# Expert loop of a mixture-of-experts layer: rows gathered in quarters, block transposes on VectorE, weight rows loaded in a matching order

## The chip, the cores and the metric

The kernel runs on one core of a Trainium2 chip. Its time is the device time of one execution in microseconds (us), median of several runs.

## The reference

One layer on 1024 tokens of width 1024, all in float32. A dense part (modulation from `c`, RMSNorm, an input projection, a gated linear recurrence, a spatial gating unit, an output projection) gives `h`. Then a mixture of 32 experts, 4 per token:

```
logits = hf @ router_w + router_b;  top 4 of 32, softmax over the four = gates
gu = xb @ w_gu[e] + b_gu[e]                    # xb: the rows of expert e, w_gu[e]: 1024 x 2048
g, lin = split(gu); g = min(g, 7); lin = clip(lin, -7, 7)
act = g * sigmoid(1.702 * g) * (lin + 1)
y = act @ w_down[e] + b_down[e]                # w_down[e]: 1024 x 1024
out[token] += y * gate
```

The sum is scaled by `g2`, added to `h`, and a last RMSNorm follows. The weights of the experts are 32 x (8 + 4) MiB = 402.65 MB; each expert's are read once.

## The kernel before

The dense part fills the first part of the run. At its end the router's results give a list of **items**: one item is up to 128 rows of one expert, cut into up to four **units** of 32 rows. With the reference's inputs the 32 experts have 8, 8, 5, 10, 4, 8, 7, 5, 3, 4, 1, 2, 2, 2, 3, 3, 5, 1, 4, 2, 4, 3, 4, 3, 5, 5, 2, 3, 4, 5, 12 and 6 units: 143 units in 47 items (so 15 items beyond the first of an expert, in 13 of the experts). Each engine runs a loop over the 47 items.

**TensorE, one item.** Weights are the moving operand, and a unit's 32 rows are the stationary one, so four 32-column matmuls stand side by side in the array, each on another quarter of the output columns. `gate_and_linear(u, half)` (line 1117) multiplies unit `u` with the slabs 0 to 3 or 4 to 7 of `w_gu` (a slab is 128 rows of the matrix), `down(u, ...)` (line 1143) with the eight of `w_down`. The item's 128 rows were gathered from `hs_rows` as whole rows of 4 KB, so they stand with tokens on partitions: `transpose_rows` (line 1084) turns them by eight TensorE transposes into PSUM, and ScalarE's `modulate` (line 780) drains them into `izT` with scale and shift. The activation of a unit is turned the same way (`transpose_act`, line 1129, drained by `drain_at`, line 792). `make_list` (line 1062) finds the tokens of an item by a product with a one-hot matrix, `repeat_rows` (line 1071) copies token number and gate to the four quarters of the partitions.

**VectorE** reads the list (`read_list`), builds the one-hot matrix (`make_onehot`, line 1567), adds biases and clamps (lines 1620 to 1628), multiplies the activation (line 1631) and scales the result (lines 1636, 1639). **ScalarE** takes the sigmoid (line 787). **GpSimd** issues the gather of the next item (line 577), multiplies gate and sigmoid (line 594), and issues per unit a scatter that adds into `acc_rows` (line 587), each behind the landing of the one before.

**SyncE** loads the weights. All 12 loads of an expert are 1 MiB: eight slabs of `w_gu` (`chunk_source`, rows `q*128` to `q*128+127`), then four of `w_down` with two slabs each. There is room for one expert's weights alone, so the loads are released in three groups by `freed[0..2]`, counted in items: the slabs 0 to 3 when the first matmul of the second half of the expert's last item has run, the slabs 4 to 7 with the first `down` of that item, the down slabs with the `repeat_rows` behind its last `down`. The loads of the first expert start within the dense part: slabs 6 and 7 and the down slabs come last of them. At the very start SyncE issues eleven small loads of parameters (line 395), each a matrix of so many rows of 128 numbers, one row per partition:

```
PARAM_ROWS = [("c", 8), ("norm1_g", 8), ("norm2_g", 8), ("conv_b", 4), ("lru_br", 4), ("lru_bi", 4),
              ("lru_lambda", 4), ("gnorm_lru_g", 4), ("gnorm_sgu_g", 4), ("conv_w", 16), ("ada_b", 48)]
```

Of the kernel before, what the change touches and what calls it, by code (L numbers as in the profile page):

```python
# [14 lines left out]
BF16 = mybir.dt.bfloat16  # L15
# [46 lines left out]
CHUNKS = 12  # L62
# [3 lines left out]
BIAS = 768  # L66

# [65 lines left out]
def build(nc, ins, out):  # L133
# [8 lines left out]
    with ExitStack() as ctx:  # L142
# [37 lines left out]
        zg = r2[:, 0:1024]  # L180
        izT = r2[:, 1024:2048].rearrange("p (k n) -> p k n", k=KT)
        actT = r2[:, 2048:3072].rearrange("p (u h n) -> p u h n", u=UMAX, h=2)
        act_sb = r2[:, 3072:3584].rearrange("p (b n) -> p b n", b=2)
        gate_sb = r2[:, 3584:4096].rearrange("p (b n) -> p b n", b=2)
        lin_sb = r2[:, 4096:4608].rearrange("p (b n) -> p b n", b=2)
        sig_sb = r2[:, 4608:5120].rearrange("p (b n) -> p b n", b=2)
        gsig_sb = r2[:, 5120:5632].rearrange("p (b n) -> p b n", b=2)
        y_sb = r2[:, 5632:6656].rearrange("p (u n) -> p u n", u=UMAX)
        bias_rows = r2[:, 8192:8192 + 2 * BIAS]
        onehot = r2[:, 9728:10240].bitcast(BF16).rearrange("p (t n) -> p t n", t=TT)  # L190
        repeat = r2[:, 10240:10752].rearrange("p (u i n) -> p u i n", u=UMAX, i=4)
        g2_rows = r2[:, 10752:11008]
        lgT_sb = r2[0:NE, 12288:13312]
# [26 lines left out]
        scale2 = sb("scale2", [P, KT])  # L220
# [18 lines left out]
        slot_c = sb("slot_c", [P, 2])  # L239
        quarter = sb("quarter", [P, 1])  # L240
        lst = g1row[:, 372:378]
        lst_t = g1row[:, 380:384]
        cur6 = g1row[:, 384:408].bitcast(BF16).rearrange("p (t i) -> p t i", t=TT)
        row_gate = g1row[:, 408:410]
        idx_next = sb("idx_next", [P, 1], I32)
        sidx_next = sb("sidx_next", [P, UMAX], I32)
        sidx_cur = sb("sidx_cur", [P, UMAX], I32)
        sgate_next = g1row[:, 416:420]
        sgate_cur = g1row[:, 420:424]
# [61 lines left out]
        pair_made = sem("pair_made")  # L311
        freed = [sem(f"freed{c}") for c in range(3)]
        z1_made = sem("z1_made")
        z2_made = sem("z2_made")
        z1_drained = sem("z1_drained")
        z2_drained = sem("z2_drained")
# [9 lines left out]
        at_drained = sem("at_drained")  # L326
# [63 lines left out]
        def _(sp_):  # L390
# [25 lines left out]

            def bias_in_rows(e):
# [11 lines left out]
            for q in range(CHUNKS):  # L429
# [7 lines left out]
                if q == 10:  # L437
                    sp_.wait_ge(filled, JOB[("rank", 0)] + 1)
                sp_.dma_start(chunk_tile(q), chunk_source(0, q)).then_inc(w_arrived[q], SEMW)
# [3 lines left out]
            for e in range(1, NE):  # L443
                done = sp_.value_load(items_i[0:1, CUM_ITEMS + e - 1:CUM_ITEMS + e], min_val=1, max_val=MAX_ITEMS)
                for q in range(CHUNKS):
                    if q % 4 == 0:
                        sp_.wait_ge(freed[q // 4], done)
                    sp_.dma_start(chunk_tile(q), chunk_source(e, q)).then_inc(w_arrived[q], SEMW)
# [25 lines left out]
        def _(pool):  # L474
            chain = [0]

            def link(ins_):
# [22 lines left out]
            link(pool.iota(tokpart[:, :, 0], pattern=[[1, TT]], base=-TT, channel_multiplier=0,  # L500
                           allow_small_or_imprecise_dtypes=True))
            link(pool.iota(tokpart[:, :, 1], pattern=[[0, TT]], base=0, channel_multiplier=1,
                           allow_small_or_imprecise_dtypes=True))
            link(pool.memset(tokpart[:, :, 2], 1.0))
            link(pool.iota(slot_c[:, 0:1], pattern=[[0, 1]], base=S, channel_multiplier=1,
                           allow_small_or_imprecise_dtypes=True))
            link(pool.iota(slot_c[:, 1:2], pattern=[[0, 1]], base=0, channel_multiplier=-1,
                           allow_small_or_imprecise_dtypes=True))
            for i in range(4):
                link(pool.memset(quarter[32 * i:32 * i + 32, :], float(i)))  # L510
# [1196 lines left out]
```

## Time and profile before

| what | value |
|---|---|
| median of 3 runs | 2426.13 us (2425.0 to 2430.72) |
| the profiled execution | 2432.23 us, its span 2430.5 us |
| granted TensorE clock, mean | 0.947 |
| TensorE matmuls busy | 2136.2 us, 88% of the span |
| VectorE, ScalarE, GpSimd busy | 769.7, 388.2, 440.6 us |
| moved by DMA | 525.82 MB, mean 216 GB/s |

The span is cut into 40 slices in the profile. The expert loop fills it from 523.5 us (the first matmul of line 1117) to 2398.3 us. Times below are microseconds from the start of the span. A TensorE instruction on float32 leaves two records, so 32 matmuls of a unit with `w_gu` stand as 64.

### The profile page before, as it was taken

Reading aid. Unit: us, or ns where it says so; the run is one execution under the profiler, and the core shown is the slowest. Engines: PE = TensorE matmul, PEld = TensorE weight load, DVE = VectorE, ACT = ScalarE, POOL = GpSimd, SP = SyncE. Lnnn points to the kernel's source line nnn. Section 1 sums busy time; section 2 is a strip of 40 time slices with the busy share of each in tenths; the row PEclk is TensorE's granted clock in tenths of the full one; section 3 lists DMA queues with packets and bytes.
Section 4 is the critical chain, followed back from the end, with each engine's and each line's share of the span. In section 5 each row is a group of like instructions: output and inputs, shape, how many; then the busy total and the mean of one; then the engine's idle time right before and its main releaser. Section 6 shows DMA issues by size and latency. Waiting matters only on the chain.

```text
span 2430.5 us, 53256 instructions
## 1 busy us (share of the span) xinstructions
PE 2136.2 (88%) x21037; PEld 924.2 (38%) x21038; DVE 769.7 (32%) x2033; ACT 388.2 (16%) x866; POOL 440.6 (18%) x420
## 2 busy tenths in 40 slices
PE   3998989959998999999796799797898889989994
PEld 3443444424433343443343233333343333433342
DVE  6437554232222232222222222222222222222223
ACT  3044112211011111101011101101101111010112
POOL 2000030112222121221211111111121111122121
PEclk9999999969999999999898899898999989999997
DMA  9312224323464357436799997699787549944245
GB/s 337 121 39 104 104 113 164 105 93 123 132 242 163 96 189 286 147 110 237 251 366 369 401 398 277 247 388 356 270 317 264 204 167 406 360 132 160 88 162 166
DMA packets 142462, 525.82 MB, mean 216 GB/s; under 512 B 14672, under 2 KB 45376, under 8 KB 109664
## 3 DMA queue, kind: packets, MB, share of 16 engines
q1 hardware_dynamic: 111728, 470.39, 49.9%
q0 software_dynamic: 30704, 55.06, 10.2%
q8 instruction: 15, 0.25, 0.0%
q14 instruction: 15, 0.12, 0.0%
HBM read 493.02 MB, written 32.37 MB: 216 GB/s over the span
## 4 chain that ended last, share of the span: by engine, by line
PE 58%; DMA 19%; issue 9%; DVE 6%; SPq 2%; ACT 2%; POOL 2%; POOLq 1%; DVEq 0%; ACTq 0%
PE psum L1117 29%; PE psum L1143 12%; DMA acc_rows<-r,sidx_cur 10%; PE psum L1013 4%; PE psum L880 4%; DMA r<-hs_rows,idx_next 4%; DMA big<-in_exp_w_gu_dram 3%; PE psum L975 2%; PE psum L1084 1%; PE psum L1129 1%; DMA big<-in_w_in_dram 1%; PE psum L1071 1%; POOL r L594 1%; PE psum L922 1%; DMA big<-in_exp_w_down_dram 1%
## 5 line engine op out<-in xcount | busy, mean ns | idle before, releaser
L1117 PE MATMUL psum<-big,r 128*32 128x512 f32 x9152 | 1022.0, 600 | 23.5 <-DMA big<-in_exp_w_gu_dram 23.0
L1143 PE MATMUL psum<-big,r 128*32 128x256 f32 x9152 | 529.2, 385 | 17.2 <-issue 14.2
L1117 PEld LDWEIGHTS psum<-big,r 128*32 128x32 f32 x9152 | 286.5, 111 | 675.7 <-issue 632.0
L1143 PEld LDWEIGHTS psum<-big,r 128*32 128x32 f32 x9152 | 293.7, 111 | 227.6 <-issue 54.2
L587 POOL DMA_INDIRECT acc_rows<-r,sidx_cur x143 | 229.0, 1601 | 804.8 <-DMA acc_rows<-r,sidx_cur 435.6
L787 ACT ACTIVATE r<-r 128x256 f32<-128x256 f32 x143 | 59.4, 416 | 1252.7 <-DVE r L1626 1252.7
L594 POOL TENSOR_TENSOR r<-r 128x256 f32<-128x256 f32 x143 | 104.5, 731 | 647.9 <-ACT r L787 647.8
L1620 DVE TENSOR_TENSOR r<-psum,r 128x256 f32<-128x256 f32 x143 | 60.7, 425 | 505.3 <-PE psum L1117 505.3
L1636 DVE TENSOR_TENSOR r<-psum,r 128x256 f32<-128x256 f32 x143 | 60.8, 425 | 437.0 <-PE psum L1143 437.0
L1084 PE MATMUL psum<-ident,r 128*128 128x128 f32 x384 | 70.7, 315 | 129.1 <-DMA r<-hs_rows,idx_next 129.1
L880 PE MATMUL psum<-r,big 128*128 128x512 f32 x384 | 167.8, 597 | 1.5 <-DMA big<-in_w_in_dram 1.5
L780 ACT ACTIVATE r<-psum,mod,scale 128x128 f32<-128x128 f32 x384 | 142.1, 461 | 28.0 <-PE psum L1084 28.0
L1631 DVE TENSOR_TENSOR r<-r 128x256 f32<-128x256 f32 x143 | 60.8, 425 | 215.9 <-POOL r L594 215.9
L792 ACT ACTIVATE r<-psum 128x256 f32<-128x256 f32 x143 | 55.3, 386 | 377.1 <-PE psum L1129 377.1
L1084 PEld LDWEIGHTS psum<-ident,r 128*128 128x128 f32 x384 | 50.4, 160 | 169.5 <-DMA r<-hs_rows,idx_next 142.7
L1013 PE MATMUL psum<-big,r 128*128 128x512 f32 x256 | 111.1, 594 | 0.5 <-DMA big<-in_w_out_dram 0.3
L880 PEld LDWEIGHTS psum<-r,big 128*128 128x128 f32 x384 | 73.2, 191 | 92.9 <-issue 91.2
L1013 PEld LDWEIGHTS psum<-big,r 128*128 128x128 f32 x256 | 48.3, 190 | 62.5 <-issue 61.3
L1639 DVE SCALAR_TENSOR_TENSOR r<-r,g1row 128x256 f32<-128x256 f32 x143 | 69.5, 486 | 5.1
L1129 PE MATMUL psum<-ident,r 128*128 128x128 f32 x286 | 63.0, 304 | 6.6 <-DVE r L1631 6.6
L1268 DVE SCALAR_TENSOR_TENSOR gacc<-big,cact,gacc 128x512 f32<-128x512 f32 x84 | 63.2, 752 | 3.0
L577 POOL DMA_INDIRECT r<-hs_rows,idx_next x48 | 48.7, 1015 | 69.0 <-DVE idx_next L1587 44.0
(233 smaller groups left out, 1122.5 us busy)
## 6 DMA issues: line engine op xcount, KB each, us to landing
big<-in_exp_w_gu_dram SPq DMA_DIRECT2D x256, 1024.0 KB
big<-in_exp_w_down_dram SPq DMA_DIRECT2D x128, 1024.0 KB
big<-in_ada_w_dram SPq DMA_DIRECT2D x12, 2048.0 KB, 12.9
r<-in_x_dram SPq DMA_DIRECT2D x16, 512.0 KB, 12.5
big<-in_w_in_dram SPq DMA_DIRECT2D x4, 2048.0 KB, 19.1
r<-in_exp_b_gu_dram SPq DMA_DIRECT2D x128, 64.0 KB
big<-in_w_out_dram SPq DMA_DIRECT2D x2, 2048.0 KB, 13.3
hs_rows<-r POOLq DMA_DIRECT2D x8, 512.0 KB, 3.2
```

Source lines behind the costliest of these rows:

```text
L587: pool.indirect_dma_start(acc_quarters, bass.IndirectOffsetOnAxis(ap=sidx_cur[:, u:u + 1], axis=0), y_sb[:, u, :], None, bounds_check=4 * ...
L594: pool.tensor_tensor(gsig_sb[:, u % 2, :], gate_sb[:, u % 2, :], sig_sb[:, u % 2, :], ALU.mult).then_inc(gsig_made, 1)
L780: ins_ = act.activation(izT[:, k, :], psum[:, 6 + half, i * P:(i + 1) * P], ACT.Identity, bias=mod[:, SH2 + k:SH2 + k + 1], scale=scale2[: ...
L880: last = pe.matmul(b, w[:, k, m * P:(m + 1) * P], zT[:, k, th * 512:(th + 1) * 512], start=(k == 0), stop=(k == KT - 1))
L1013: last = pe.matmul(b, src[:, ct % CT, t * P:(t + 1) * P], ring(("wout", dh))[:, ct, :], start=(ct == 0), stop=(ct == 2 * CT - 1))
L1084: last = pe.transpose(psum[:, 6 + half, i * P:(i + 1) * P], zg[:, k * P:(k + 1) * P], ident[:, :])
L1117: last = pe.matmul(psum[32 * j:32 * j + 32, u, :].rearrange("p (a n) -> p a n", a=2), izT[:, k, u * UNIT:(u + 1) * UNIT], rhs[:, :, 256 * ...
L1129: last = pe.transpose(psum[:, u, h * P:(h + 1) * P], act_sb[:, u % 2, h * P:(h + 1) * P], ident[:, :])
L1143: ins_ = pe.matmul(psum[32 * i:32 * i + 32, 4 + u % 2, 0:256], actT[:, u, h, 32 * j:32 * j + 32], down_slab(f)[:, 256 * i:256 * i + 256], ...
L1268: ins_ = dve.scalar_tensor_tensor(out=a, in0=w[:, k, :], scalar=cact[:, k:k + 1], in1=a, op0=ALU.mult, op1=ALU.add)
L1631: dve.tensor_tensor(act_sb[:, u % 2, :], lin_u, gsig_sb[:, u % 2, :], ALU.mult).then_inc(act_made, 1)
L1639: dve.scalar_tensor_tensor(out=y_sb[:, u, :], in0=y_sb[:, u, :], scalar=sgate_cur[:, u:u + 1], in1=g2_rows, op0=ALU.mult, op1=ALU.mult).th ...
```

## The change

- A weight slab is now rows `k*32` to `k*32+31` of each of the four quarters of the matrix (`j` = 0 to 3 on partitions `32j` to `32j+31`), not 128 rows that follow each other. The source of a load has the shape 4 x 32 x 2048 (or 1024), the destination 128 partitions. The down slabs are loaded one by one: 16 loads per expert in place of 12.
- The gather of an item is four indirect DMAs, each of 128 quarter rows of 1 KB: partition `32i + n` of unit `u` gets quarter `i` of token `n`'s row. VectorE turns each 32 x 32 block of it by one instruction (`block_rows`), and ScalarE's `modulate` reads SBUF, with scale and shift rearranged once to match (`shift2`).
- Gate times sigmoid moves from GpSimd to VectorE, and a second block transpose there makes the operand of `down`; `transpose_rows`, `transpose_act` and `drain_at` are gone.
- Lists are made three items ahead and gathers issued two ahead; the scatters of an item no longer wait for each other, only for those of the item before.
- The slabs 4 to 7 are released by the first matmul of `make_list`, which now stands ahead of the `down` products.

```diff
-CHUNKS = 12
+CHUNKS = 16
...
         def chunk_tile(q):
-            if q < 8:
-                return gu_slab(q)
-            at = (q % 2) * 2048
-            return big[:, SLOT_OF_PAIR[q // 2], at:at + 2048].rearrange("p (k n) -> p k n", k=2)
+            return gu_slab(q) if q < 8 else down_slab(q - 8)
         def chunk_source(e, q):
             if q < 8:
-                return w_gu[e, q * P:(q + 1) * P, :]
-            return w_down[e, (q - 8) * 256:(q - 7) * 256, :].rearrange("(k p) n -> p k n", p=P)
+                return w_gu[e].rearrange("(j k r) n -> k j r n", j=4, k=KT)[q]
+            return w_down[e].rearrange("(j k r) n -> k j r n", j=4, k=KT)[q - 8]
...
+            def load_chunk(e, q):
+                sp_.dma_start(chunk_tile(q), chunk_source(e, q)).then_inc(w_arrived[q], SEMW)
...
+            def gather(turn, step):
                 pool.wait_ge(idx_made, turn + 1)
+                if not (isinstance(turn, int) and turn == 0):
+                    pool.wait_ge(z_blocked, turn)
                 pool.sem_inc(may_start, 1)
-                pool.indirect_dma_start(zg, None, hs_rows, bass.IndirectOffsetOnAxis(ap=idx_next[:, 0:1], axis=0)
-                                        ).then_inc(rows_in, SEMW)
+                step(pool.tensor_copy(gather_idx[:, :], quarter_of[:, bass.ds(turn * UMAX, UMAX)]))
+                pool.sem_inc(may_start, 1)
+                for u in range(UMAX):
+                    pool.indirect_dma_start(z_quarters[:, u, :], None, hs_quarters,
+                                            bass.IndirectOffsetOnAxis(ap=gather_idx[:, u:u + 1], axis=0)
+                                            ).then_inc(rows_in, SEMW)
...
+            def block_rows(turn):
+                dve.wait_ge(rows_in, turn * (UMAX * SEMW) + UMAX * SEMW)
+...
                dve.transpose(z_blocks.rearrange("p u k n -> p (u k n)"), z_quarters.rearrange("p u n -> p (u n)")
+                              ).then_inc(z_blocked, 1)
...
+                    dve.tensor_tensor(gsig_sb[:, u % 2, :], gate_u, sig_sb[:, u % 2, :], ALU.mult).then_inc(gsig_made, 1)
 XX_tensor(act_sb[:, u % 2, :], lin_u, gsig_sb[:, u % 2, :], ALU.mult).then_inc(act_made, 1)
+                    dve.transpose(actT[:, u, :, :].rearrange("p k n -> p (k n)"), act_sb[:, u % 2, :]).then_inc(at_made, 1)
...
-                transpose_rows(g + 1, 0)
-                transpose_act(0)
...
+                make_list(g + 3)
+                down(0)
                 load_item(g + 1)
```

SyncE's queue, the loads of the second expert. Before:

```order
L448 DMA big<-in_exp_w_gu_dram 128x2048 x4
L422 DMA r<-in_exp_b_gu_dram 32x2x256
L425 DMA r<-in_exp_b_down_dram 32x256
L422 DMA r<-in_exp_b_gu_dram 32x2x256
L425 DMA r<-in_exp_b_down_dram 32x256
L422 DMA r<-in_exp_b_gu_dram 32x2x256
L425 DMA r<-in_exp_b_down_dram 32x256
L422 DMA r<-in_exp_b_gu_dram 32x2x256
L425 DMA r<-in_exp_b_down_dram 32x256
L448 DMA big<-in_exp_w_gu_dram 128x2048 x4
L448 DMA big<-in_exp_w_down_dram 128x2x1024 x4
```

With the change:

```order
L421 DMA big<-in_exp_w_gu_dram 128x1x2048 x4
L428 DMA r<-in_exp_b_gu_dram 32x2x256
L431 DMA r<-in_exp_b_down_dram 32x256
L428 DMA r<-in_exp_b_gu_dram 32x2x256
L431 DMA r<-in_exp_b_down_dram 32x256
L428 DMA r<-in_exp_b_gu_dram 32x2x256
L431 DMA r<-in_exp_b_down_dram 32x256
L428 DMA r<-in_exp_b_gu_dram 32x2x256
L431 DMA r<-in_exp_b_down_dram 32x256
L421 DMA big<-in_exp_w_gu_dram 128x1x2048 x4
L421 DMA big<-in_exp_w_down_dram 128x1x1024 x8
```

The shapes are those of the destination; the order is the same, and the down slabs are eight loads.

TensorE, from the second half of an item's first unit to its first `down` product. Before:

```order
L1117 MATMUL psum<-big,r 32x512 x16
L350 UNCONDITIONAL_BRANCH
L1079 ISA
L1084 MATMUL psum<-ident,r 128x128 x4
L1107 REGISTER_ALU
L1129 MATMUL psum<-ident,r 128x128 x2
L348 COMPARE_AND_BRANCH
L348 UNCONDITIONAL_BRANCH
L1117 MATMUL psum<-big,r 32x512 x16
```

With the change:

```order
L1101 MATMUL psum<-big,r 32x512 x16
L355 UNCONDITIONAL_BRANCH x3
L1049 REGISTER_ALU
L1051 REGISTER_ALU
L1053 MATMUL psum<-g1row,r 128x6 x8
L1091 REGISTER_ALU
L1119 MATMUL psum<-big,r 32x256 x32
```

No transposes stand between the products any more, and the list's product stands ahead of `down`.

VectorE, one unit's activation. Before:

```order
L1620 TENSOR_TENSOR r<-psum,r 128x256
L1622 ISA
L1622 SCALAR_TENSOR_TENSOR r<-psum,r 128x256
L1626 TENSOR_SCALAR r<-r 128x256
L1628 TENSOR_SCALAR r<-r 128x256
L1631 TENSOR_TENSOR r<-r 128x256
```

With the change:

```order
L1585 TENSOR_TENSOR r<-psum,r 128x256
L1587 SCALAR_TENSOR_TENSOR r<-psum,r 128x256
L1591 TENSOR_SCALAR r<-r 128x256
L1593 TENSOR_SCALAR r<-r 128x256
L1596 TENSOR_TENSOR r<-r 128x256
L1598 TENSOR_TENSOR r<-r 128x256
L1600 STREAM_TRANSPOSE r<-r 128x256
```

The rows L1596 and L1600 are new on this engine.

## Rows read from the trace of the kernel before

**Rows 1.** The page: span and busy time.
```profile
span 2430.5 us, 53256 instructions
```
**Rows 2.** Groups by line on PE: shapes xcount | busy us, mean ns | idle before, releasers.
```profile
L1117 PE MATMUL psum<-big,r 128*32 128x512 f32 x9152 | 1022.0, 600 | 23.5 <-DMA big<-in_exp_w_gu_dram 23.0 <-issue 0.5
L1143 PE MATMUL psum<-big,r 128*32 128x256 f32 x9152 | 529.2, 385 | 17.2 <-issue 14.2 <-DMA big<-in_exp_w_down_dram 2.8
...
L1084 PE MATMUL psum<-ident,r 128*128 128x128 f32 x384 | 70.7, 315 | 129.1 <-DMA r<-hs_rows,idx_next 129.1
...
L1129 PE MATMUL psum<-ident,r 128*128 128x128 f32 x286 | 63.0, 304 | 6.6 <-DVE r L1631 6.6
```
**Rows 3.** Stretches: busy us per engine, PEclk, DMA share of 16 engines, GB/s.
```profile
530.00:2400.00 1870.00, 1696.69 (x19674) 712.57 (x19666) 494.49 (x1601) 241.32 (x662) 378.59 (x331) 0.96 0.66 238
```
**Rows 4.** Timeline of an undisturbed stretch: start, us, engine, line.
```profile
1112.85 7.11 PE L1143 MATMUL psum<-big,r 128*32 128x256 f32 x128 [0.33 <-issue]
...
1119.90 1.05 PE L1071 MATMUL psum<-g1row,r 128*128 128x2 f32 x8
...
1121.08 20.81 PE L1117 MATMUL psum<-big,r 128*32 128x512 f32 x192
```
**Rows 5.** DMA queues and issues, whole span.
```profile
q1 hardware_dynamic: 111728, 470.39, 49.9%
q0 software_dynamic: 30704, 55.06, 10.2%
...
big<-in_exp_w_gu_dram SPq DMA_DIRECT2D x256, 1024.0 KB
big<-in_exp_w_down_dram SPq DMA_DIRECT2D x128, 1024.0 KB
```
**Rows 6.** DMA in the first 10 us: packets by size, and four of the loads.
```profile
DMA packets 857, 1.42 MB, mean 142 GB/s; under 512 B 80, under 2 KB 192, under 8 KB 857
...
r<-in_norm_g_dram SPq DMA_DIRECT2D x2, 4.0 KB
r<-in_ada_b_dram SPq DMA_DIRECT2D x1, 24.0 KB
...
r<-in_conv_b_dram SPq DMA_DIRECT2D x1, 2.0 KB
...
r<-in_conv_w_dram SPq DMA_DIRECT2D x1, 8.0 KB
```
**Rows 7.** Stretch in which four slabs of weights land, columns as in rows 3.
```profile
604.00:608.00 4.00, 3.67 (x70) 2.03 (x64) 0.91 (x2) 0.07 (x1) 0.33 (x1) 1.00 1.01 426
```
**Rows 8.** Timeline of SyncE: last loads of expert 0, three groups of expert 1.
```profile
477.53 16.51 SPq L439 DMA_DIRECT2D big<-in_exp_w_down_dram  x4
...
586.02 2.10 SPq L448 DMA_DIRECT2D big<-in_exp_w_gu_dram  x4
...
601.72 2.13 SPq L448 DMA_DIRECT2D big<-in_exp_w_gu_dram  x4
617.06 2.02 SPq L448 DMA_DIRECT2D big<-in_exp_w_down_dram  x4
```
**Rows 9.** A two-unit item: stretch as in rows 3, and a TensorE wait.
```profile
1340.00:1365.00 25.00, 19.02 (x179) 5.96 (x171) 5.34 (x16) 4.18 (x12) 4.03 (x4) 0.86 1.03 407
...
1349.13 1.94 PE L1117 MATMUL psum<-big,r 128*32 128x512 f32 x8 [2.03 <-DMA big<-in_exp_w_gu_dram]
```
**Rows 10.** Timeline: the last work of the loop on TensorE.
```profile
2398.19 1.05 PE L1071 MATMUL psum<-g1row,r 128*128 128x2 f32 x8
```
**Rows 11.** Groups by line on DVE and POOL, columns as in rows 2.
```profile
L594 POOL TENSOR_TENSOR r<-r 128x256 f32<-128x256 f32 x143 | 104.5, 731 | 647.9 <-ACT r L787 647.8
...
L1631 DVE TENSOR_TENSOR r<-r 128x256 f32<-128x256 f32 x143 | 60.8, 425 | 215.9 <-POOL r L594 215.9
...
L1567 DVE TENSOR_TENSOR r<-r 128x1024 bf16 x49 | 60.1, 1226 | 3.1
...
L1395 DVE TENSOR_REDUCE r<-big 128x512 f32<-128x2048 f32 x3 | 10.9, 3669 | 2.0 <-ACT big L697 2.0
```

More of the change, by code:

```diff
@@ L66 @@
 BIAS = 768
+LISTS = MAX_ITEMS + 3
 def bank_jobs():
@@ L310, in build @@
         may_start = sem("may_start")
-        pair_made = sem("pair_made")
+        copy_made = sem("copy_made")
+        rows_repeated = sem("rows_repeated")
+        rows_taken = sem("rows_taken")
+        z_blocked = sem("z_blocked")
         freed = [sem(f"freed{c}") for c in range(3)]
[L313 to L316, printed above, removed]
+        z_made = [sem(f"z_made{c}") for c in range(2)]
+        affine2_made = sem("affine2_made")
+        shift2_made = sem("shift2_made")
         gu_made = sem("gu_made")
@@ L325, in build @@
         at_made = sem("at_made")
-        at_drained = sem("at_drained")
         dn_made = sem("dn_made")
@@ L609, in gsig_2 @@
-                def gsig_2():
-                    times_sigmoid(prior, 2)
-                    by_units(pool, units, 3, gsig_3)
-                def gsig_1():
-                    times_sigmoid(prior, 1)
-                    by_units(pool, units, 2, gsig_2)
-                by_units(pool, units, 1, gsig_1)
+                gather(g + 2, step)
+                pool.wait_ge(acc_out, prior * SEMW + SEMW * TT)
+                pool.sem_inc(may_start, 1)
+                step(pool.tensor_copy(scatter_idx[:, :], quarter_of[:, bass.ds(g * UMAX, UMAX)]))
@@ L737, in _ @@
             group_root(1, 1)
+            act.wait_ge(affine2_made, 1)
+            for j in range(4):
+                for q in range(4):
+                    ins_ = act.activation(shift2[32 * j:32 * j + 32, :, :].rearrange("p a (h q) -> p a h q", h=2)[:, :, :, q],
+                                          affine2[32 * q:32 * q + 32, :, 2 * j:2 * j + 2], ACT.Copy)
+            ins_.then_inc(shift2_made, 1)
             def norm_h(t):
@@ L775, in modulate @@
             def modulate(turn, half):
-                act.wait_ge((z1_made, z2_made)[half], turn + 1)
-                for i in range(4):
-                    k = 4 * half + i
-                    ins_ = act.activation(izT[:, k, :], psum[:, 6 + half, i * P:(i + 1) * P], ACT.Identity,
-                                          bias=mod[:, SH2 + k:SH2 + k + 1], scale=scale2[:, k:k + 1])
-                ins_.then_inc((z1_drained, z2_drained)[half], 1)
+                act.wait_ge(z_blocked, turn + 1)
+                for k in range(4 * half, 4 * half + 4):
+                    ins_ = act.activation(izT[:, k, :].rearrange("p (u n) -> p u n", u=UMAX), z_blocks[:, :, k, :],
+                                          ACT.Identity, bias=shift2[:, 1, k:k + 1], scale=shift2[:, 0, k:k + 1])
+                ins_.then_inc(z_made[half], 1)
             def sigmoid(prior, u):
@@ L1591, in _ @@
+            def block_rows(turn):
+                dve.wait_ge(rows_in, turn * (UMAX * SEMW) + UMAX * SEMW)
+                if not (isinstance(turn, int) and turn == 0):
+                    dve.wait_ge(z_made[0], turn)
+                    dve.wait_ge(z_made[1], turn)
+                dve.transpose(z_blocks.rearrange("p u k n -> p (u k n)"), z_quarters.rearrange("p u n -> p (u n)")
+                              ).then_inc(z_blocked, 1)
+            TAKE_STEPS = 5
             dve.wait_ge(gates_made, 1)
```

286 lines of the change are left out of this document (122 added, 164 removed).

## The prediction

> **What bounds the kernel now.** I read the groups by line first. TensorE is busy nearly all the time: the two expert products take 1022.0 and 529.2 us, and the transposes that the change removes take 70.7 + 63.0 us and have 129.1 + 6.6 us of waiting ahead of them, nearly all for the gather [rows 2]. The windows say the same of the loop: in 1870 us TensorE is busy 1697, VectorE 494, and the DMA engines 0.66 of their time [rows 3]. So the loop is bound by TensorE, but not by far: a DMA share of 0.66 with all 16 engines at work means that the weights could stand a slowdown of 1.5 and no more. In a two-unit item they bind already: the share is 1.03 at 407 GB/s, and TensorE waits 2.03 us for one slab [rows 9].
>
> So the first question is not what the transposes cost but whether the weights still come as fast. They are 402.65 MB, 384 loads of 1 MiB [rows 5].
>
> **How a load is spread over the engines.** The first 10 us show eleven small loads: three of 8 rows (`c` and the two norms), six of 4 rows (as `conv_b`), one of 16 (`conv_w`), one of 48 (`ada_b`) [rows 6]. Their data are 112 packets of 512 B, which is 192 - 80 in the packet line; the 80 packets under 512 B are their completions, one per engine that took part [rows 6]. Eleven loads on 16 engines each would leave 176. 3 x 8 + 6 x 4 + 16 + 16 = 80 fits exactly. So a load whose outermost count is 4 ran on four engines, one of 8 on eight, one of 48 on sixteen. Before the change every weight load has 128 outermost on both sides. With it the source is 4 x 32 x 2048: the outermost count is 4 on the source's side, 128 on the destination's. No row shows such a mixed pair. Either the smaller one decides, and a load has 4 engines, or the larger, and it has 16. I take 4: a share for an engine must be cut from both sides alike, and 4 blocks that do not follow each other cannot be cut 16 ways along their outermost step.
>
> The Trainium skill states this as a rule ("DMA: Bandwidth & Descriptors", "Why a DMA increments its semaphore by 16 and not by 1"): the largest number up to 16 that divides the slowest dimension of both sides, and from SyncE the lowest-numbered engines. By that rule, with which the 80 completions agree, the weight loads all share the same four. Which engines a load takes, no row here shows.
>
> **The sum if a weight load has four engines.**
> - The rate of one engine: 426 GB/s at a share of 1.01 of 16 [rows 7] is 26.4 GB/s, so four give 105.4. The lower bound is the mean of the whole queue, 470.39 MB in 49.9% of 16 engines' 2430.5 us [rows 5, 1], 24.2 GB/s. I take 26.4, since it comes from weight slabs alone.
> - One expert is 12.583 MB: 119.4 us. TensorE needs (6.94 + 3.56) us per unit (20.81 / 3 and 7.11 / 2 [rows 4]), 47 us for the mean expert of 4.5 units. So the queue of weights becomes the path. Only the largest expert, 12 units or 126 us, computes as long as one load takes.
> - Expert 0: its last loads are issued about 477 us [rows 8]; two slabs of 1 MiB and eight of half a MiB then take 60 us. Its weights are there at 540.
> - Experts 1 to 31: 31 x 119.4 = 3701 us.
> - Holds. A single-item expert doesn't hold the queue: slab 4 arrives, the second half starts and frees the next expert's first group while the down slabs still come. With more items, that group is freed only in the last item, so the queue stands while TensorE does the down products of units 2 to 4 (10.7), the list (1.2) and the first half of the last item (3.47 per unit). That is 15.4 for each of six experts of 5 units, 22 for 7, 26 for each of three of 8, and 62 and 69 for those of 10 and 12 with a middle item of 43: 322 us. The last expert's rest is 34, and the twelve restarts cost 20 (some 1.5 us each: a group issued at 601.72 moves at its full rate by 604 [rows 7, 8]). Together 376.
> - Other traffic on these four engines: GpSimd's queue takes 10.2% of 16 engines' span [rows 5, 1], so 248 us of each one's time. Its part before the loop doesn't count, bias loads and quartered gathers add about as much. I take 248; bounds 0 (all within the holds) and 400.
> - TensorE's granted clock: it fell to 0.86 on the mean of the stretch with slab waits [rows 9], so half level for a part of it. In 14 exposed stretches I add some 3 us each: 40. At none of the others does its speed matter.
> - The end of the loop to the end of the span: 2430.5 - 2398.3 = 32 [rows 1, 10].
>
> 540 + 3701 + 376 + 248 + 32 + 40 = 4937 us of span. The profiled execution was 1.7 us over its span and 6.1 over the median of the runs shown, so I forecast 4933.
>
> The Trainium skill gives about 27 GiB/s per engine (same page, "Specifications"), 29 GB/s. By that an expert would take 108.5 us and the sum would be 4600; the row's 26.4 is what this chip shows, and stands.
>
> **What the rest of the change does.** In this case nothing of it shows: everything below lies beside the weights. The transposes leave TensorE (134 us busy), which then waits for slabs instead; the stall for the gather goes, because the rows have 120 us to come; what is late next is always a slab. On VectorE a 128x1024 block transpose per item and a 128x256 one per unit are new and no row has their price. Between the 1226 ns of a two-operand pass over 128x1024 and the 3669 ns of a reduction over 2048 columns [rows 11] I take 1.2 us and a fourth of it, nearest in kind, with 0.43 us for gate times sigmoid, which took 731 ns on GpSimd [rows 11]: 48 x 1.2 + 143 x 0.75 = 165 us on an engine that is busy 494 of 1870 [rows 3]; at three times the price 300. Four gathers instead of one cost GpSimd 3 us more per item, on an engine with 1491 idle us. The entry of the loop makes three lists in place of one, some 5 us, and ScalarE's 16 small copies for `shift2` about 4 us; both lie ahead of expert 0's slabs and hide behind them.
>
> **The rivals.**
> *The larger count decides (16 engines): faster.* Against it speaks the argument above, for it nothing but that no row shows a mixed pair. Then the loop's 1875 us lose 134 + 136 of transposes and waits [rows 2] and some 25 of the lighter `repeat_rows`. Of this the weights take back about 45 (an expert cannot be shorter than 12.583 MB / 407 GB/s = 31 us, and five of one or two units would be 9 us shorter), and the chain of activation and VectorE transpose behind one-unit items about 35, ten times 3.5: 2430.5 - 295 + 80 = 2215. It decides if a load leaves 16 completions. Lower end 2160, where nothing is taken back.
> *Four engines per load, but not always the same four: faster, less so.* Four loads in flight would then still use all 16. The whole rate stays, a slab alone takes 10 us instead of 2.5, which costs some 7 us at each of about ten places where TensorE meets a fresh group: 2290. The 80 completions allow it.
> *As forecast, but the four engines share badly with GpSimd's queue.* A scatter has rows on all 16 and waits behind 8 KB packets on four; slower by up to 150 more. It is within the range.
>
> **How the numbers follow.** Four fixed engines 0.82, sixteen 0.12, four in turn 0.05, something between 0.01. A measurement of this kernel can tell about 0.3%, 7 us, from no change, and every case is far outside: slower 0.82, faster 0.17, same 0.01. The likeliest case's bounds: below, no cost of other traffic or clock and half of the holds, 4937 - 248 - 40 - 190 = 4459; above, 24.2 GB/s per engine (129.8 us per expert, 322 more) and 150 for the sharing, 5409. The range is 4450 to 5450; it leaves out the two faster cases and little else, about 2 in 10. Taking them in would make it reach over two thousand us in which I expect nothing.
>
> **What would show it.** In the packets: 512 weight loads leave 4 completions each. In the windows of the loop: a DMA share near 0.25 to 0.3 and about 105 GB/s, flat from expert to expert, and a span of some 120 us per expert whatever its units. In the groups by line: lines 1101 and 1119 wait for `in_exp_w_gu` and `in_exp_w_down` for over 2000 us in all, TensorE is busy about 2000 us and its clock is below 0.9. If instead the slabs come at over 400 GB/s, the forecast is wrong at its one decisive step, and the time is near 2215.

## The result, and the profile after the change

| | before | with the change |
|---|---|---|
| median, device us (4 runs each) | 2427.74 (2425.0 to 2430.72) | 4938.2 (4934.7 to 4941.42) |
| profiled span | 2430.5 | 4937.3 |
| granted TensorE clock, mean | 0.947 | 0.695 |

The ratio is 2.034, 95% interval 2.0305 to 2.0375: the change makes the kernel take twice as long. The forecast was 4933.

The page of the changed kernel: span, busy time per engine, packets, queues, chain by engine, and groups in the form of [rows 2, 11].

```profile
span 4937.3 us, 51646 instructions
PE 2417.8 (49%) x20191; PEld 813.1 (16%) x20192; DVE 940.1 (19%) x2237; ACT 359.1 (7%) x739; POOL 516.5 (10%) x527
...
DMA packets 140863, 526.35 MB, mean 107 GB/s; under 512 B 12944, under 2 KB 43648, under 8 KB 108064
...
q1 hardware_dynamic: 107632, 470.37, 23.9%
q0 software_dynamic: 33200, 55.60, 5.4%
...
SPq 57%; DMA 17%; PE 14%; issue 1%; DVE 0%; ACT 0%; DVEq 0%; POOLq 0%
...
L1101 PE MATMUL psum<-big,r 128*32 128x512 f32 x9152 | 1279.7, 711 | 1648.3 <-DMA big<-in_exp_w_gu_dram 1646.2
L1119 PE MATMUL psum<-big,r 128*32 128x256 f32 x9152 | 692.3, 453 | 735.9 <-DMA big<-in_exp_w_down_dram 691.4
...
L591 POOL DMA_INDIRECT r<-hs_rows,gather_idx x196 | 212.5, 1084 | 89.5 <-issue 47.6
...
L1596 DVE TENSOR_TENSOR r<-r 128x256 f32<-128x256 f32 x143 | 60.9, 426 | 53.8 <-ACT r L798 53.8
...
L1600 DVE STREAM_TRANSPOSE r<-r 128x256 f32<-128x256 f32 x143 | 63.7, 445 | 4.9
L1546 DVE STREAM_TRANSPOSE r<-r 128x1024 f32<-128x1024 f32 x48 | 59.8, 1246 | 22.9 <-DMA r<-hs_rows,gather_idx 12.0
```

The two products now wait 1646.2 + 691.4 us for weights, against 23.0 + 2.8 before [rows 2]. Nothing else grew like this: VectorE has its new transposes and is busy 19%, and the 129.1 us wait for the gather is gone, with the instruction that had it. The queue of weights moved the same 470.4 MB as in [rows 5], but with 23.9% of sixteen engines' time in twice the span.

Two windows of the changed kernel, the whole loop and one stretch in which an expert's weights come, columns as in [rows 3]:

```profile
530.00:4900.00 4370.00, 1981.17 (x18736) 602.37 (x18732) 657.33 (x1788) 207.26 (x514) 445.51 (x423) 0.67 0.28 102
2500.00:2620.00 120.00, 43.50 (x364) 11.95 (x368) 14.01 (x38) 4.43 (x11) 9.49 (x9) 0.60 0.30 112
```

The DMA view of 2600 to 2700 us in 40 slices: tenths of sixteen engines that are busy, and GB/s. It is flat but for its last slice.

```profile
DMA  2222222222222222222222222222222222222225
GB/s 105 105 105 107 94 97 105 108 105 105 111 108 105 105 105 108 105 105 111 106 102 105 105 105 105 105 105 105 105 105 105 105 105 105 105 105 110 105 108 144
```

SyncE's timeline, from the first loads of one expert to those of the next two, experts of three units and less (start, time of the issues, count; the rows of SyncE's other loads are left out):

```profile
2427.07 22.95 SPq L421 DMA_DIRECT2D big<-in_exp_w_gu_dram  x4
...
2472.91 22.81 SPq L421 DMA_DIRECT2D big<-in_exp_w_gu_dram  x4
2495.77 54.42 SPq L421 DMA_DIRECT2D big<-in_exp_w_down_dram  x8
...
2551.31 22.96 SPq L421 DMA_DIRECT2D big<-in_exp_w_gu_dram  x4
...
2675.89 22.97 SPq L421 DMA_DIRECT2D big<-in_exp_w_gu_dram  x4
```

From one expert to the next it is 124.24 and 124.58 us. Four issues took about 2 us in [rows 8] and now take 23, and eight take 54: by these times the queue is full and takes a load only when an older one has gone. That is what "SPq 57%" in the chain is.

The **completions** give the number of engines. Under 512 B there were 14672 packets before and 12944 now. 384 weight loads with 16 completions each left 6144; 512 with 4 each leave 2048, so 4096 fewer. The gathers are 196 instructions instead of 48, 16 completions each: 2368 more. 14672 - 4096 + 2368 = 12944, to the packet.

### The profile page after: what moved, and what is told of

The parts are those of the page before. It is cut to its first block, busy times and chain, and to the rows that moved or that the text cites. A ratio compares the mean times of both kernels' runs of the same rounds, so it can differ in the third digit from the quotient of the medians.

```text
span 4937.3 us, 51646 instructions
## 1 busy us (share of the span) xinstructions
PE 2417.8 (49%) x20191; PEld 813.1 (16%) x20192; DVE 940.1 (19%) x2237; ACT 359.1 (7%) x739; POOL 516.5 (10%) x527
## 2 busy tenths in 40 slices
DMA packets 140863, 526.35 MB, mean 107 GB/s; under 512 B 12944, under 2 KB 43648, under 8 KB 108064
## 3 DMA queue, kind: packets, MB, share of 16 engines
q1 hardware_dynamic: 107632, 470.37, 23.9%
## 4 chain that ended last, share of the span: by engine, by line
SPq 57%; DMA 17%; PE 14%; issue 1%; DVE 0%; ACT 0%; DVEq 0%; POOLq 0%
SPq L421 45%; DMA big<-in_exp_w_down_dram 17%; PE psum L1119 9%; SPq L428 6%; SPq L431 5%; PE psum L1101 5%; DVE r L1650 0%; DVE r L1605 0%; SPq L459 0%; DMA r<-hs_rows,gather_idx 0%; DMA acc_rows<-r,scatter_idx 0%; DMA r<-acc_rows 0%; PE psum L1065 0%; PE psum L1053 0%; SPq L450 0%
## 5 line engine op out<-in xcount | busy, mean ns | idle before, releaser
L1101 PE MATMUL psum<-big,r 128*32 128x512 f32 x9152 | 1279.7, 711 | 1648.3 <-DMA big<-in_exp_w_gu_dram 1646.2
L1119 PE MATMUL psum<-big,r 128*32 128x256 f32 x9152 | 692.3, 453 | 735.9 <-DMA big<-in_exp_w_down_dram 691.4
L599 POOL DMA_INDIRECT acc_rows<-r,scatter_idx x143 | 226.5, 1584 | 3702.8 <-DVE r L1608 3683.2
L791 ACT ACTIVATE r<-r,shift 128x128 f32<-128x128 f32 x384 | 157.3, 480 | 2968.1 <-PE psum L1101 2672.3
L591 POOL DMA_INDIRECT r<-hs_rows,gather_idx x196 | 212.5, 1084 | 89.5 <-issue 47.6
L1596 DVE TENSOR_TENSOR r<-r 128x256 f32<-128x256 f32 x143 | 60.9, 426 | 53.8 <-ACT r L798 53.8
L1600 DVE STREAM_TRANSPOSE r<-r 128x256 f32<-128x256 f32 x143 | 63.7, 445 | 4.9
L1546 DVE STREAM_TRANSPOSE r<-r 128x1024 f32<-128x1024 f32 x48 | 59.8, 1246 | 22.9 <-DMA r<-hs_rows,gather_idx 12.0
L1517 DVE TENSOR_TENSOR r<-r 128x1024 bf16 x50 | 61.3, 1225 | 4.2
L1598 DVE TENSOR_TENSOR r<-r 128x256 f32<-128x256 f32 x143 | 60.8, 425 | 4.9
L1587 DVE SCALAR_TENSOR_TENSOR r<-psum,r 128x256 f32<-128x256 f32 x143 | 59.2, 414 | 0.0
```

The source lines that it names most:

```text
L591: pool.indirect_dma_start(z_quarters[:, u, :], None, hs_quarters, bass.IndirectOffsetOnAxis(ap=gather_idx[:, u:u + 1], axis=0)).then_inc(r ...
L599: pool.indirect_dma_start(acc_quarters, bass.IndirectOffsetOnAxis(ap=scatter_idx[:, u:u + 1], axis=0), y_sb[:, u, :], None, bounds_check=4 ...
L791: ins_ = act.activation(izT[:, k, :].rearrange("p (u n) -> p u n", u=UMAX), z_blocks[:, :, k, :], ACT.Identity, bias=shift2[:, 1, k:k + 1] ...
L1101: last = pe.matmul(psum[32 * j:32 * j + 32, u, :].rearrange("p (a n) -> p a n", a=2), izT[:, k, u * UNIT:(u + 1) * UNIT], rhs[:, :, 256 * ...
L1119: ins_ = pe.matmul(psum[32 * i:32 * i + 32, 4 + u % 2, 0:256], actT[:, u, f, :], down_slab(f)[:, 256 * i:256 * i + 256], start=(f == 0), s ...
L1600: dve.transpose(actT[:, u, :, :].rearrange("p k n -> p (k n)"), act_sb[:, u % 2, :]).then_inc(at_made, 1)
```

## The experiments

The theory: a weight load is cut by the smaller of the two outermost counts, which is 4, and always onto the same four engines; everything else of the change hides or helps. Rivals: the same four are not always used; or the rest of the change (order of rows, transposes on VectorE, gathers) carries a part of the loss. Where a time below stands without an interval, it is that of one execution; the effects there are hundreds of us, but small differences can't be read from it.

### One matrix in the kernel before

```diff
-                return w_gu[e, q * P:(q + 1) * P, :]
+                return w_gu[e].rearrange("(j k r) n -> k j r n", j=4, k=KT)[q]
```

> The kernel before with one line changed: a w_gu slab is rows of the four quarters of the matrix, source 4 x 32 x 2048 in place of 128 x 2048. Its rows then don't match the activations', so the output is another; the w_down loads, the transposes and the gather are those of before. Theory (a load runs on as many engines as the smaller outermost count): w_gu comes at 105 GB/s, 79.6 us per expert, w_down at 407 GB/s, 10.3: 90 us per expert, 31 x 90 + 510 + 376 of holds + some 200 of other traffic + 72 = about 3950 us; 4 completions per w_gu load. Rival (the loss comes from the rest of the change: VectorE's transposes, gathers of quarters, order of lists): 2430 us.

The second run has `j=8`.

> As the run with 4 x 32, with the source as 8 x 16 x 2048 (rows k*16 to k*16+15 of each eighth of the matrix; again other rows than the reference's). Theory: eight engines, w_gu at 211 GB/s, 39.8 + 10.3 = 50 us per expert, which is more than TensorE's work for experts of up to four units and less for the others: between 2700 and 3000 us, 8 completions per load. Rival (the rows being apart in HBM costs, not the number of engines): as slow as with 4 x 32. Rival (loss elsewhere in the change): 2430 us.

Measured: **4359.67 us** with 4 blocks, **3373.58 us** with 8 (before on this chip: 2433.01). The packets lines, of 4 blocks and then of 8:

```profile
DMA packets 139390, 525.81 MB, mean 121 GB/s; under 512 B 11600, under 2 KB 42304, under 8 KB 106592
```
```profile
DMA packets 140414, 525.81 MB, mean 156 GB/s; under 512 B 12624, under 2 KB 43328, under 8 KB 107616
```

14672 - 11600 = 3072 = 256 x 12 and 14672 - 12624 = 2048 = 256 x 8: each of the 256 loads lost 12 and 8 of its 16 completions. The cut is shown, without anything else of the change. Windows in which only `w_gu` comes, of 4 blocks and of 8:

```profile
2040.00:2060.00 20.00, 8.46 (x52) 1.81 (x48) 0.00 (x0) 0.00 (x0) 0.00 (x0) 0.65 0.26 106
```
```profile
1505.00:1530.00 25.00, 24.48 (x320) 10.99 (x316) 8.40 (x27) 5.89 (x16) 4.52 (x5) 0.99 0.57 210
```

106 GB/s on four engines, 210 on eight. Both times are above what I expected (3950, and 2700 to 3000). Single-item experts took about 102 and 65 us, where I had 90 and 50. The sum had overlooked what happens when `w_down` comes beside `w_gu`. SyncE issues the two kinds one after the other, and the next `w_gu` only from 2086.14; the row and the packets of 2074 to 2076 us in the run with 4 blocks stand behind the issues:

```profile
2033.79 22.27 SPq L448 DMA_DIRECT2D big<-in_exp_w_gu_dram  x4
2056.10 29.23 SPq L448 DMA_DIRECT2D big<-in_exp_w_down_dram  x4
...
2074.00:2076.00 2.00, 0.00 (x0) 0.00 (x0) 0.00 (x0) 0.00 (x0) 0.00 (x0) 0.50 1.04 258
...
DMA packets 114, 0.52 MB, mean 258 GB/s; under 512 B 1, under 2 KB 1, under 8 KB 101
```

A row of `w_gu` is a packet of 8 KB and one of `w_down` a packet of 4 KB, so 13 packets of `w_gu` and 100 of `w_down` moved in these 2 us: loads issued later run beside the earlier ones, on the engines that those leave free. All sixteen are then busy, but at 258 GB/s and not at the 407 that I had taken for `w_down`; with 8 blocks it is 240 at a share of 1.00 (1535 to 1540 us). Why the two kinds slow each other was not tried, nor how much of the 400 us it explains.

### The same four engines?

The changed kernel, each slab as two loads of 64 partitions, so with two outermost blocks each:

```diff
-                sp_.dma_start(chunk_tile(q), chunk_source(e, q)).then_inc(w_arrived[q], SEMW)
+                for j in (0, 2):
+                    sp_.dma_start(chunk_tile(q)[32 * j:32 * j + 64, :], chunk_source(e, q)[j:j + 2]
+                                  ).then_inc(w_arrived[q], SEMW)
```

> The changed kernel with each slab loaded by two loads of 64 partitions, source 2 x 32 rows. Same bytes, same order of rows, same result. Theory with fixed, lowest engines: each load runs on two engines and the two loads of a slab on the same two: 239 us per expert, 31 x 239 + 600 + 376 + some 400 of other traffic: about 8800 us. Rival (a load has few engines, but another set each time): the two loads in flight use four or more engines together, 4940 us or less.

Measured: **8678.18 us**. Its window of the loop:

```profile
600.00:8500.00 7900.00, 1975.14 (x17924) 575.61 (x17924) 624.45 (x1698) 197.13 (x489) 429.50 (x407) 0.59 0.15 56
```

Two loads that follow each other share two engines; the share of 0.15 is two of sixteen and the gathers. There are again 12944 packets under 512 B: 1024 loads with 2 completions each leave as many as 512 with 4. If the two loads went to different engines, they would run beside each other, as `w_gu` and `w_down` do above, and the time would have stayed below 4940. So loads with the same count use the same engines, and the rate goes with their number: 56, 105 and 210 GB/s at two, four and eight (the 56 with the gathers' traffic).

### Four loads of one block each

A block of 32 rows is contiguous, so its outermost count is 32 on both sides:

```diff
+                for j in range(4):
+                    sp_.dma_start(chunk_tile(q)[32 * j:32 * j + 32, :], chunk_source(e, q)[j]).then_inc(w_arrived[q], SEMW)
```

> The changed kernel with each slab loaded by four loads of 32 partitions, source 32 rows that follow each other; 64 loads per expert. Same result. Theory: 32 outermost on both sides gives 16 engines, and the rest of the change shows: about 2215 us (2160 to 2290), 16 completions per load. SyncE's issue, 64 x 0.43 + 4 = 32 us per expert, is as long as an expert's bytes take (31 us), so it may show in the experts of one and two units. Rival (the four-block pattern is not the cause): near 4938 us. Rival (VectorE and the gathers cost more than the transposes did): over 2430 us.

Measured: **2868.55 us**, ratio 1.1801 (1.1768 to 1.1835). All sixteen engines are back (43664 small packets = 12944 + 2048 x 16 - 2048), and 2070 us of the loss are gone. But the expectation of 2215 missed by 650. A window:

```profile
1300.00:1400.00 100.00, 54.85 (x540) 16.71 (x536) 24.47 (x67) 8.04 (x21) 16.39 (x16) 0.68 1.04 233
```

The share is 1.04 and yet only 233 GB/s move, where [rows 7] had 426 at 1.01. Busy engines are not enough: each is at half its rate. The new theory: 32 partitions reach only half of the ways into SBUF. The Trainium skill says so ("SBUF — State Buffer", "Door 1: The DMA port swizzle"): 32 partitions reach 8 of 16 ports, 64 no more than 32, and a port carries about 27 GB/s, so 218 at most; the 233 of the window, in which GpSimd's packets are too, is a little above that. Rivals: the rows' order in DRAM, 64 issues per expert, or the rest of the change. Four runs tell them apart.

### Interleaved rows: whole loads, and still a block transpose

If slab `k` holds the rows `8p + k`, then `p` is one step of the address, so both sides have 128 outermost and a load is one load of 128 partitions. The block transpose then reads every eighth column:

```diff
-                return w_gu[e].rearrange("(j k r) n -> k j r n", j=4, k=KT)[q]
-            return w_down[e].rearrange("(j k r) n -> k j r n", j=4, k=KT)[q - 8]
+                return w_gu[e].rearrange("(p k) n -> k p n", k=KT)[q]
+            return w_down[e].rearrange("(p k) n -> k p n", k=KT)[q - 8]
...
-                    dve.transpose(actT[:, u, :, :].rearrange("p k n -> p (k n)"), act_sb[:, u % 2, :]).then_inc(at_made, 1)
+                    dve.transpose(actT[:, u, :, :], act_sb[:, u % 2, :].rearrange("p (r k) -> p k r", k=KT)).then_inc(at_made, 1)
```

> The change, with another order of the weight rows that also matches a block transpose: slab k holds the rows 8p + k, so a load is 128 x 2048 with 128 outermost on both sides and is still one load of 128 partitions. The block transposes read their input with a stride to match, and scale and shift are rearranged through a small matrix in DRAM. Theory (the whole loss is the number of engines a load is cut over, and in the run with four loads of 32 partitions the rest was the reach of a 32-partition destination): a load leaves 16 completions, the loop's full stretches run at 400 GB/s or more, an 8 KB packet is back at about 309 ns, and the time is what the prediction gave for sixteen engines, 2215 us (2160 to 2290), faster than both kernels. Rival (the rest of the change has a price of its own, VectorE's strided transposes, or gathers that take the queue's time): 2400 us or more, with TensorE waiting for VectorE or GpSimd and not for weights.

Measured: **2238.82 us**, ratio 0.9206 (0.9194 to 0.9219), faster than both kernels, 24 us from the 2215 that the prediction gave for sixteen engines. Windows (the loop, and a stretch of loads) and groups of this kernel:

```profile
530.00:2200.00 1670.00, 1565.14 (x18739) 615.91 (x18735) 710.56 (x1787) 207.41 (x514) 463.49 (x423) 0.97 0.74 267
602.00:606.00 4.00, 3.70 (x72) 2.30 (x72) 0.91 (x2) 0.00 (x0) 1.63 (x1) 1.00 1.01 424
```
```profile
L1103 PE MATMUL psum<-big,r 128*32 128x512 f32 x9152 | 1025.2, 605 | 52.2 <-DMA big<-in_exp_w_gu_dram 45.8 <-issue 6.3
L1121 PE MATMUL psum<-big,r 128*32 128x256 f32 x9152 | 532.6, 389 | 45.5 <-issue 19.4 <-DVE r L1602 18.7 <-DMA big<-in_exp_w_down_dram 7.0
```

424 GB/s with rows that are 64 KB apart: that rows do not follow each other costs nothing. TensorE is busy 94% of the loop. So the whole loss of the change was the cut of the weight loads; without it, the rest of the change gains 193 us.

### Half the rate: destination, number of loads, or rows?

The kernel before, its own order of rows, each `w_gu` slab as four loads of 32 partitions:

> The kernel before with its own order of rows, but each w_gu slab is issued as four loads of 32 partitions x 2048; w_down as it was. Theory (a load of 32 partitions writes at about half the rate whatever rows it reads): w_gu then comes at about 233 GB/s, 36 us per expert, and w_down at over 400, 10 us, together 46 plus 5 of other traffic, which is near what TensorE needs for the mean expert, so the large experts hide part of it: about 2650 us (2500 to 2800). Rival (the order of the rows in DRAM made the packets slow in the run with four loads of the change, not the destination): the same time as before, 2430 us, within 1%.

The changed kernel, each pair of slabs as four loads of 32 partitions, quarters in the order 0, 2, 1, 3:

> The change, each pair of slabs as four loads of 32 partitions x 2 slabs, in the order of quarters 0, 2, 1, 3: 24 loads per expert instead of 64 in the run with four loads per slab. Theory (each load is limited by the reach of its 32 partitions, and the loads of a queue follow each other on all engines in step): still about 230 to 240 GB/s and about 2850 us. Rival A (the number of loads and completions cost the time): the loads fall to 3/8, so the rate rises, to 2500 us or less. Rival B (neighbouring loads overlap, so that two halves of the partitions are written at once when the quarters alternate): over 350 GB/s, 2250 to 2400 us.

Measured: **2836.97 us** (ratio 1.1664, 1.1643 to 1.1685) and **2791.09 us**. In the kernel before with four loads, a stretch of `w_gu` and one of `w_down`:

```profile
1520.00:1530.00 10.00, 7.09 (x100) 3.53 (x96) 3.10 (x13) 0.00 (x0) 1.60 (x1) 0.99 1.01 224
1560.00:1565.00 5.00, 4.98 (x32) 1.26 (x36) 1.58 (x5) 0.42 (x1) 0.72 (x1) 0.61 1.03 410
```

The same queue, a few us apart: 224 GB/s into 32 partitions, 410 into 128. Neither the order of the rows nor anything else of the change is in this kernel, so the destination is left, or the number of loads. Against the number speaks the share of 1.01: the engines don't stand between loads, each packet takes longer. This kernel's time is 190 above my 2650, where I had counted on large experts to hide part of it. By SyncE's timeline an expert of five units took 102.8 us, against 82.1 before: the slabs are freed only by its last item, so a large expert pays as the small ones do. The pairs (24 loads in place of 64) are 77 us faster than four loads per slab, and stretches of 5 us lie between 230 and 405 GB/s. The fastest of them:

```profile
1570.00:1575.00 5.00, 3.97 (x48) 2.00 (x52) 0.91 (x2) 0.00 (x0) 1.56 (x1) 0.74 1.01 405
```

Every weight load of this kernel goes to 32 partitions, so two loads to different halves must overlap here, and together they get nearly the rate of 128; most stretches stay near 240. Whether the order of the quarters or the smaller number of loads gave the 77 us stays open. The time of the pairs is between my cases and nearest to the first, so neither rival holds.

### Sixteen blocks, far apart and near

The kernel before with 16 blocks of 8 rows to 128 partitions; in the first run 64 rows apart (`j=16` in the edit of the first run), in the second 9:

```diff
-                return w_gu[e, q * P:(q + 1) * P, :]
+                return w_gu[e, q * 120:q * 120 + 144, :].rearrange("(j r) n -> j r n", j=16)[:, 0:8, :]
```

> The kernel before with the source of each w_gu load as 16 x 8 x 2048, the blocks of 8 rows 64 rows apart; it computes with wrong rows of w_gu. Theory (only the outermost count decides the engines; rows that do not follow each other cost nothing): 16 completions per load, the packets line of the profile as before, 2430 us within 1%. If rows apart cost something of their own, or a split source makes the packets slower as in the run with 8 x 16 (432 ns for 8 KB instead of 309): well over 2430, at 432 ns up to 2900 us.

> As the run with 16 x 8, but the blocks of 8 rows lie 9 rows apart instead of 64, so the source is nearly as contiguous in DRAM as before the change and still three dimensions deep; wrong rows of w_gu again. The run with 16 x 8 kept 16 engines and still took 2821 us at about 230 GB/s. Theory (the cut gives each engine 8 partitions that follow each other, and then the engines write half of the ways into SBUF at a time): the same as with 64 rows apart, 2820 us within 1%. Rival (rows that lie 512 KB apart in DRAM collide there): near 2430 us, since the rows are near each other now.

Measured: **2820.54 us** (ratio 1.1611, 1.1593 to 1.163) and **2810.37 us** (1.1591, 1.1543 to 1.1639). The packets line is that of before in both, 14672 under 512 B, so sixteen engines; and yet, in the first and in the second:

```profile
1520.00:1530.00 10.00, 3.00 (x16) 0.36 (x16) 2.68 (x11) 0.00 (x0) 0.48 (x1) 0.67 1.02 230
```
```profile
1525.00:1530.00 5.00, 5.00 (x34) 1.15 (x28) 0.00 (x0) 0.00 (x0) 0.70 (x1) 0.66 1.00 228
```

The expectation that only the number of engines counts fell with the first run, and the second excludes the distance in DRAM. That the source has three dimensions is no sufficient cause either: with 4 blocks it has them too, and each of its four engines moved the full 26.4 GB/s. The likeliest cause left is which partitions an engine writes. The Trainium skill points to a reason ("DMA: Bandwidth & Descriptors", "The descriptor swizzle"): in a 128-partition transfer an engine writes partitions that share one port, such as 0 to 3 and 32 to 35, and sixteen engines use sixteen ports. If a cut in 16 blocks gives an engine 8 partitions in a row, four of them lie on one port and four on the next, and while all engines walk through the first four, only every second port is used. Half of the ports would give 218 GB/s by the Trainium skill's figure above (an estimate), and the rows show 228 and 230. But this is not shown. No row tells which partitions an engine writes, and the four-block load speaks against the picture as it stands: if its engines had 32 partitions in a row each, two of them would meet on one port (0 to 3 and 32 to 35) while they walk in step, and give half of the 105 GB/s that were measured. Why 16 blocks run at half rate and 4 at full rate per engine stays open.

### What the other 193 us are

The kernel before with one line of the change, scatters that don't wait for each other:

```diff
-                pool.wait_ge(acc_out, prior * SEMW + (SEMW * u + SEMW * TT))
+                if u == 0:
+                    pool.wait_ge(acc_out, prior * SEMW + SEMW * TT)
```

> The kernel before, with the one line of the change that lets the scatters of an item go without waiting for each other. Before, GpSimd's next gather stands behind the last of them, and in the chain of waits each costs 8.4 us and the gather 5.1 us. Theory (TensorE's 129 us of waiting ahead of its transposes comes from the gather being behind the scatters): for items of four units two waits of 9 us less each, so nearly all of that stall goes, 2430 down to 2310 (2290 to 2350). Rival (the stall is the gather's own latency, one item ahead is too late in any case): under 40 us of gain, 2390 us or more.

The interleaved kernel with that wait restored, and with gate times sigmoid back on GpSimd:

> The change with interleaved rows (2239 us), with the scatters of an item waiting for each other again as before the change. Theory (gathers two items ahead have room for it): within 0.5% of 2239 us. Rival (the free scatters are what removed the stall, in this kernel too): 2280 us or more, with TensorE or VectorE waiting for the gathered rows.

> The change with interleaved rows (2239 us), with gate times sigmoid back on GpSimd. VectorE's strided block transposes took more than forecast there (2.08 and 0.65 us), and TensorE waited 18.7 us for the transposed activation. The move to VectorE costs VectorE 0.43 us a unit and saves 0.73 on GpSimd and one hand-over. Theory (the chain behind the last unit decides, and it is shorter on one engine): 5 to 25 us slower than 2239. Rival (VectorE is the late engine, so relieving it helps): faster, 2225 us or less.

Measured, with 2428.82 for the kernel before: **2362.01 us** (0.9727, 0.9706 to 0.9748), **2244.56 us** (0.9249, 0.9227 to 0.927) and **2254.7 us** (0.9287, 0.9268 to 0.9305). The chain of waits of the kernel before shows what the first takes away; scatters in a row, then the gather that TensorE waits for:

```profile
1626.37 8.38 DMA acc_rows<-r,sidx_cur
...
1635.59 8.40 DMA acc_rows<-r,sidx_cur
...
1646.19 8.47 DMA acc_rows<-r,sidx_cur
...
1657.70 5.10 DMA r<-hs_rows,idx_next
```

With free scatters (groups of TensorE):

```profile
L1118 PE MATMUL psum<-big,r 128*32 128x512 f32 x9152 | 1024.5, 601 | 33.6 <-DMA big<-in_exp_w_gu_dram 33.0 <-issue 0.5
...
L1085 PE MATMUL psum<-ident,r 128*128 128x128 f32 x384 | 68.4, 307 | 55.0 <-DMA r<-hs_rows,idx_next 55.0
```

The wait fell from 129.1 to 55.0 us, not to nearly nothing, and 10 us came back as a wait for weights: 67 us of gain where I expected 119. So both theories hold in part: the scatters ahead of the gather cost some 70 us, and a gather one item ahead is too late at times even without them. The two runs of the interleaved kernel were on another chip than its own 2238.82, so I compare ratios to the kernel before: the same wait costs 0.3 to 0.5% (the two intervals just part), as expected of gathers two items ahead. Gate times sigmoid is better on VectorE, by 0.7 to 0.9%, 16 to 20 us; the group of `down` in that run shows where they went:

```profile
L1141 PE MATMUL psum<-big,r 128*32 128x256 f32 x9152 | 535.6, 392 | 84.0 <-DVE r L1620 63.3 <-issue 16.6 <-DMA big<-in_exp_w_down_dram 4.0
```

TensorE waits 63.3 us for the transposed activation (L1620) instead of 18.7. So a third of the 193 us can be had in the kernel before with one line; gathers two ahead and the transposes off TensorE make up the rest, and were not tried one without the other.

## Why the prediction was right, step by step

- **The cut is by the smaller outermost count.** Shown by the completions: 4 a load in the change, 4 and 8 in the single edits. The reading of 80 completions in the first 10 us [rows 6] carried the forecast.
- **The same four engines.** No row of before showed it. Shown by the run with two blocks at 8678 us, together with the `w_down` packets that overtake `w_gu`; the rival of 2290 is out.
- **26.4 GB/s per engine, 105.4 for four.** The slices read 105. It was right to take the rate of weights alone [rows 7] and not the queue's mean.
- **Experts at 119.4 us, other traffic at 248 in all.** Oversized: a single-item expert took 124.2 to 124.6 us, so 4.9 for the rest, 31 x 4.9 = 152, not 248. The rest of GpSimd's traffic probably lies within the holds; no row separates it.
- **Holds 376 and slow clock 40.** Undersized: 4937.3 - 540 - 3701 - 152 - 32 leaves 512 for both. Some 22 of the 96 too few are expert 0's. Its weights had come by 550 us (from there to 560 only 2 GB/s move), but TensorE had started on it only at 528.42 and computed without waiting for them, and the next loads were issued at 587.75: 48 us after the 540 of the sum, which had 26 for this hold.

```profile
528.42 29.64 PE L1101 MATMUL psum<-big,r 128*32 128x512 f32 x256 [2.19 <-issue]
...
587.75 11.32 SPq L421 DMA_DIRECT2D big<-in_exp_w_gu_dram  x4
```

  The others come from the stops further on. TensorE's timeline at the end of an expert of five units shows why:

```profile
2812.36 1.08 PE L1119 MATMUL psum<-big,r 128*32 128x256 f32 x8 [3.91 <-DMA big<-in_exp_w_down_dram]
2817.35 1.08 PE L1119 MATMUL psum<-big,r 128*32 128x256 f32 x8 [3.90 <-DMA big<-in_exp_w_down_dram]
2819.12 12.35 PE L1119 MATMUL psum<-big,r 128*32 128x256 f32 x192 [0.70 <-issue]
2831.40 0.25 PE L1065 MATMUL psum<-g1row,r 128*128 128x6 bf16 x4
2831.59 7.07 PE L1101 MATMUL psum<-big,r 128*32 128x512 f32 x64
```

  Windows of the same place, before and behind the stop of the queue:

```profile
2814.00:2816.00 2.00, 0.00 (x0) 0.00 (x0) 0.00 (x0) 0.00 (x0) 0.00 (x0) 0.50 0.13 53
2836.00:2840.00 4.00, 3.01 (x36) 0.82 (x28) 3.32 (x7) 1.65 (x4) 1.37 (x2) 1.00 0.30 68
```

  The weights stop at about 2815 and are not yet back at 105 GB/s at 2840, with 68 GB/s in the last row: 25 us, where the sum had 15.4 and 1.7 for the restart. It left out what lies around the products: 2.4 us from the last bytes to TensorE's start on them at 2817.35, 1.8 for the first unit's product with that slab, and about 4 from the next load's issue at 2836.1 to the full rate. And the `down` of three units took 12.35 us for its 10.7, since TensorE had been waiting most of the time and came to it at a granted clock of 0.50, the lower of its two levels (1.2 of 2.4 GHz). The two errors, 96 us down and 96 up, cancel. That the forecast lies within 0.1% is luck; either error alone would have put it 2% off.
- **The rest of the change hides.** Right. The transposes took 1246 and 445 ns, where I took 1.2 us and a fourth of it. The sixteen-engine rival's 2215 is what the interleaved kernel measured within 24 us; there the strided transposes took 18.7 us of TensorE's time in waits, and weights 52.8.

## What to carry to other kernels

Before you change the order of rows in a load, write down the outermost count of both sides: here the smaller of the two said how many DMA engines work. It is not the whole story, since 16 blocks of 8 had sixteen engines and still ran at half rate. The small-packet count of a profile tests it, because a load leaves one completion per engine. If a transpose forces an order of rows, look for one that is a single step of the address (here `8p + k` in place of `32k + r` in four quarters), and give the stride to the on-chip side, where it cost 0.8 us per 128 x 1024. And read share and GB/s together: a share of 1.0 at half the GB/s means that each packet takes twice as long.

## What was not expected of the hardware

- Loads into 32 partitions run at 224 to 233 GB/s with sixteen busy engines, against 410 to 426 into 128. Splitting a load by partitions to win engines back gave back 2070 us of 2510 and not all. Two such loads to different halves can overlap: 405 GB/s in one stretch of the run with pairs.
- Loads on four engines and loads on sixteen run beside each other from one queue, and slow each other: 258 GB/s at a share of 1.04.
- A load of 16 blocks x 8 partitions has 16 completions and runs at 228 to 230 GB/s, whether the blocks are 9 or 64 rows apart; 128 rows 64 KB apart run at 424.
- A float32 block transpose on VectorE takes 1246 ns for 128 x 1024 and 445 ns for 128 x 256 from contiguous columns, and in the interleaved kernel, reading every eighth column, 1.67 and 1.47 times as long:

```profile
L1548 DVE STREAM_TRANSPOSE r<-r 128x1024 f32<-128x1024 f32 x48 | 99.8, 2079 | 16.8 <-DVE r L1540 11.4
...
L1602 DVE STREAM_TRANSPOSE r<-r 128x256 f32<-128x256 f32 x143 | 93.5, 654 | 4.9
```
